# Two decoder layers with a mixture of experts on one core: half slots of the first gate weights get homes outside the ring

## The reference

```python
for l in range(DEPTH):                      # DEPTH = 2, SEQ = 256, D_MODEL = 1024
    h = rms_norm(x, norm_mix_g[l])
    x = x + token_mixers(h, ...)            # gMLP, sparse attention, short convolution, gated merge
    h = rms_norm(x, norm_ffn_g[l])
    x = x + hier_moe(h, ...)                # 4 groups of 8 experts, top-1 group, top-2 experts in it
return rms_norm(x, norm_final_g)

def expert_block(args):                     # one expert e, its tokens
    xb = xt[tok_b]
    hid = jax.nn.silu(xb @ w_gate[e]) * (xb @ w_up[e])   # 1024 x 512 each
    return hid @ w_down[e]                               # 512 x 1024
```

## Time and profile before

| | |
|---|---|
| median of 3 runs | 1394.22 us (1394.03 to 1395.34) |
| profiled execution | 1397.3 us, span 1395.6 us, granted clock 0.996 |
| busy share of the span | PE 98%, PEld 58%, DVE 41%, ACT 28% |
| moved by DMA | 490.27 MB, mean 351 GB/s |
| expert stage of layer 0 | PE starts it at 257.94 us |
| expert stage of layer 1 | PE starts it at 947.42 us |

### The profile page before, as it was taken

One profiled execution on the slowest core, in us unless ns is written; L12 is line 12 of the kernel. 1 busy time (PEld: TensorE's weight loads), 2 busy tenths in 40 slices (PEclk: granted clock), 3 DMA queues, 4 the chain that ended last, 5 costly groups with the idle time before them and its releaser, 6 DMA issues. The chain is left out here.

```text
span 1395.6 us, 18851 instructions
## 1 busy us (share of the span) xinstructions
PE 1366.0 (98%) x7854; PEld 810.0 (58%) x7854; DVE 574.1 (41%) x926; ACT 386.1 (28%) x709; POOL 6.3 (0%) x36
## 2 busy tenths in 40 slices
PE   8999999999999999999999999999999999999996
PEld 7899888644444444444488988884444444444332
DVE  6796646622222221212278956465222222222123
ACT  6554444211111111111164553441111111111112
POOL 0000000000000000000000000000000000000000
PEclk9999999999999999999999999999999999999999
DMA  8645757999999999999965557589999999999995
GB/s 311 218 164 185 279 199 275 403 421 428 428 428 427 426 426 428 427 427 419 405 220 184 211 188 265 189 352 386 425 428 427 427 428 427 427 427 426 426 420 243
DMA packets 86221, 490.27 MB, mean 351 GB/s; under 512 B 10303, under 2 KB 13433, under 8 KB 55417
## 3 DMA queue, kind: packets, MB, share of 16 engines
q1 hardware_dynamic: 86032, 489.03, 86.6%
q10 hardware_dynamic: 104, 0.03, 0.0%
HBM read 487.99 MB, written 1.05 MB: 350 GB/s over the span
## 5 line engine op out<-in xcount | busy, mean ns | idle before, releaser
L1984 PE MATMUL psB<-slots,uT 128*64 128x512 f32 x2048 | 459.8, 596 | 10.0 <-DMA slots<-in_expert_w_gate_dram 5.1
L1984 PEld LDWEIGHTS psB<-slots,uT 128*64 128x64 f32 x2048 | 143.7, 137 | 279.2 <-issue 275.6
L1994 PE MATMUL psC<-slots,ybT_plain 128*64 128x512 f32 x1024 | 227.2, 595 | 2.5 <-DMA slots<-in_expert_w_down_dram 1.6
L1124 DVE TENSOR_TENSOR parts<-slots,parts 128x2048 fp32r<-128x2048 f32 (+1 forms) x80 | 177.6, 2248 | 69.9 <-ACT parts L889 69.2
L889 ACT ACTIVATE parts<-slots 128x2048 fp32r<-128x2048 f32 (+1 forms) x80 | 148.3, 1888 | 97.2 <-PE psB L1653 52.7
L1500 DVE TENSOR_TENSOR x<-x,psA 128x1024 f32<-128x1024 f32 x62 | 75.7, 1221 | 227.7 <-PE psA L2031 227.7
L1994 PEld LDWEIGHTS psC<-slots,ybT_plain 128*64 128x64 f32 x1024 | 70.9, 137 | 133.3 <-issue 129.7
L996 ACT ACTIVATE rel_parts<-psC 128x512 fp32r<-128x512 f32 x62 | 37.0, 598 | 384.3 <-PE psC L1994 203.3
L1653 PE MATMUL psB<-parts,hT_parts 128*128 128x512 f32 x448 | 139.1, 392 | 1.5 <-DVE parts L1124 1.0
L1494 DVE TENSOR_TENSOR rel_parts<-psC,rel_parts 128x512 fp32r<-128x512 f32 x62 | 42.6, 688 | 163.8 <-ACT rel_parts L996 163.7
L1653 PE MATMUL psA<-parts,hT_parts 128*128 128x512 f32 x320 | 99.3, 391 | 0.0
(11 more groups left out here) (349 smaller groups left out, 1349.4 us busy)
## 6 DMA issues: line engine op xcount, KB each, us to landing
slots<-in_expert_w_down_dram SPq DMA_DIRECT2D x48, 2048.0 KB, 25.6
slots<-in_expert_w_gate_dram SPq DMA_DIRECT2D x44, 2048.0 KB, 25.7
slots<-in_expert_w_up_dram SPq DMA_DIRECT2D x44, 2048.0 KB, 24.8
slots<-in_w_in_dram SPq DMA_DIRECT2D x56, 1024.0 KB, 4.9
slots<-in_expert_w_gate_dram SPq DMA_DIRECT2D x40, 1024.0 KB, 13.0
slots<-in_expert_w_up_dram SPq DMA_DIRECT2D x40, 1024.0 KB, 13.6
slots<-in_expert_w_down_dram SPq DMA_DIRECT2D x24, 1024.0 KB, 19.1
slots<-in_w_out_dram SPq DMA_DIRECT2D x8, 1024.0 KB, 4.9
```

The lines of the kernel that those rows point to most:

```text
L1124: v.tensor_tensor(low_part, mix_slot(i), high_part, ALU.subtract).then_inc(low_dve, 1)
L1984: ins = te.matmul(psB[j * BLK:(j + 1) * BLK, o, :], xT[:, 4 * half + c, j * BLK:(j + 1) * BLK], w[:, c, :], start=half == 0 and c == 0, st ...
L1994: ins = te.matmul(psC[j * BLK:(j + 1) * BLK, n, :], hidT[:, 2 * k + c, j * BLK:(j + 1) * BLK], w[:, c, n * 512:(n + 1) * 512], start=k == ...
```

## The change

Three halves of gate slots of pair 0 get homes outside the ring: half 0 of load 0 in a new tile `first_rows`, half 0 of load 2 in `rel`, half 1 of load 3 in `ybT`. The freed half slots (half 0 of slots 0 and 2, half 1 of slot 3) take half of the down weights of pair 1 (loads 20, 22, 23). Stage 0 of pair 0 uses the chunks in the order 2, 3, 0, 1. `load_raw(35)` moves ahead of the wait for `merged_done`. The throw-away squares go to `uT`.

```diff
+        FIRST = {0: (sb("first_rows", [P, SLOT // 2]), 0),
+                 2: (nc.alloc_sbuf_tensor_at("first_in_rel", [P, SLOT // 2], F32, offset=place["rel"][0]), 0),
+                 3: (nc.alloc_sbuf_tensor_at("first_in_ybT", [P, SLOT // 2], F32, offset=place["ybT"][0]), 1)}
...
+                def load_first(n):
+                    home, piece = FIRST[n]
+                    load_piece(n, experts_of(0), home[:, :], piece, first_landed[n])
+                def load_early(s):
+                    n, piece = SLOTS + s, FIRST[s][1]
+                    load_piece(n % PAIR_SLOTS, experts_of(n // PAIR_SLOTS), half_slot(s, piece), piece, early_landed[s])
+                def load_rest(n):
+                    piece = 1 - FIRST[n % SLOTS][1]
+                    load_piece(n % PAIR_SLOTS, experts_of(n // PAIR_SLOTS), half_slot(n % SLOTS, piece), piece, landed[n % SLOTS])
...
                 def load_ahead(s):
...
+                    if s == 0:
+                        load_first(s)
+                    if s in FIRST:
+                        load_rest(s)
+                        return
                     load_main(s)
...
                 def load_high(i):
                     wait_used(sp, l, i)
+                    if high_slot(i) in FIRST:
+                        load_rest(high_slot(i))
+                        return
                     load_main(high_slot(i))
 
                 load_raw(MIX_SLOTS - 6)
+                wait_used(sp, l, USE[proj_of(2, 1), 0])
+                load_first(2)
+                load_raw(MIX_SLOTS - 5)
                 sp.wait_ge(merged_done, l * 2 + 2)
                 load_main(GATES_AT)
                 load_main(GATES_AT + 1)
-                load_raw(MIX_SLOTS - 5)
                 sp.wait_ge(merged_ps, l * 2 + 2)
                 load_main(MERGED_AT)
                 for i in range(MIX_SLOTS - 4, MIX_SLOTS):
                     load_high(i)
                     load_raw(i)
                 load_main(LOW_SLOT)
+                load_early(0)
+                load_early(2)
                 sp.wait_ge(route_ps, (l + 1) * NT)
                 load_main(HT_SLOT)
+                sp.wait_ge(low_x, (l + 1) * 2 * NT)
+                load_first(3)
+                load_early(3)
...
                             if n == SLOTS:
-                                load_pieces(p, experts, slots, [lambda: sp.wait_ge(early_freed, l + 1), lambda: wait_freed(n)], early_landed)
...
+                                sp.wait_ge(early_freed, l + 1)
+                                load_rest(SLOTS)
+                                load_rest(SLOTS + 2)
+                                continue
+                            wait_freed(n)
...
+                            for j in range(QB):
+                                if n + 2 * j == SLOTS + 3:
+                                    load_rest(n + 2 * j)
+                                    continue
+                                load_main(n + 2 * j)
...
-                        unread = (rel if half else uT)[:, :, :].rearrange("p h s -> p (h s)")[:, 512 * t:512 * t + 512]
+                        unread = uT[:, :, :].rearrange("p h s -> p (h s)")[:, 512 * t:512 * t + 512]
...
-                    for c in range(4):
-                        if first_pair and k == 0 and c == 2:
+                    opening = not tail and i == 0
+                    order = (2, 3, 0, 1) if opening and k == 0 else range(4)
+                    for c in order:
+                        if opening and k == 0 and c == 0:
                             ins.then_inc(early_freed, 1)
+                            pe.wait_ge(first_landed[0], (l + 1) * 16)
+                            pe.wait_ge(first_landed[2], (l + 1) * 16)
+                        if opening and k == 1 and c == 2:
+                            pe.wait_ge(first_landed[3], (l + 1) * 16)
                         for j in range(QB):
+                            home, piece = FIRST[at[j]] if opening and at[j] in FIRST else (None, None)
+                            if c // 2 == piece:
+                                w = home[:, c % 2 * 512:(c % 2 + 1) * 512]
+                            else:
+                                w = slot(at[j], SLOT)[:, c * 512:(c + 1) * 512]
...
                     if not tail and i * PAIR_SLOTS + part_of(4 + k, 0) == SLOTS:
-                        pe.wait_ge(early_landed, (l + 1) * 16 * QB)
+                        pe.wait_ge(early_landed[0], (l + 1) * 16)
+                        pe.wait_ge(early_landed[2], (l + 1) * 16)
+                    if not tail and i * PAIR_SLOTS + part_of(4 + k, 0) == SLOTS + 1:
+                        pe.wait_ge(early_landed[3], (l + 1) * 16)
```

More of the change, by code:

```diff
@@ L398, in build_trunk @@
         bidx = sb("bidx", [P, TAB_BLOCKS])
-        early_landed = sem("early_landed")
+        FIRST = {0: (sb("first_rows", [P, SLOT // 2]), 0),
+                 2: (nc.alloc_sbuf_tensor_at("first_in_rel", [P, SLOT // 2], F32, offset=place["rel"][0]), 0),
+                 3: (nc.alloc_sbuf_tensor_at("first_in_ybT", [P, SLOT // 2], F32, offset=place["ybT"][0]), 1)}
+        first_landed = {n: sem(f"first{n}_landed") for n in FIRST}
+        early_landed = {n: sem(f"early{n}_landed") for n in FIRST}
         early_freed = sem("early_freed")
@@ L625, in load_main, with experts_of, load_pieces @@
                     load_part(p, [l * NE + i * QB + j for j in range(QB)], n % SLOTS, doubled(n))
-                def load_pieces(first, experts, slots, waits, first_sem):
+                def experts_of(i):
+                    return [l * NE + i * QB + j for j in range(QB)]
+                def load_first(n):
[7 more added lines that the diff above has]
+                    load_piece(n % PAIR_SLOTS, experts_of(n // PAIR_SLOTS), half_slot(n % SLOTS, piece), piece, landed[n % SLOTS])
+                def load_pieces(first, experts, slots):
                     for piece in range(2):
-                        waits[piece]()
                         for j in range(QB):
-                            load_piece(first + 2 * j, experts, slots[j], piece, landed[slots[j]] if piece else first_sem)
+                            load_piece(first + 2 * j, experts, half_slot(slots[j], piece), piece, landed[slots[j]] if piece else tail_landed)
                 def load_ahead(s):
@@ L723, in sync_program @@
                             if k == STAGES - 1:
-                                load_pieces(part_of(k, 0), [l * NE + e for e in experts], [OVER_SLOTS[part_of(k, j)] for j in range(QB)],
-                                            [lambda: None, lambda: None], tail_landed)
+                                load_pieces(part_of(k, 0), [l * NE + e for e in experts], [OVER_SLOTS[part_of(k, j)] for j in range(QB)])
                                 continue
@@ L1977, in gate_up @@
                     at = [expert_arrived(i, part_of(k, j), tail) for j in range(QB)]
[L1978 to L1980 removed]
+                    opening = not tail and i == 0
+                    order = (2, 3, 0, 1) if opening and k == 0 else range(4)
+                    for c in order:
+                        if opening and k == 0 and c == 0:
                             ins.then_inc(early_freed, 1)
+                            pe.wait_ge(first_landed[0], (l + 1) * 16)
+                            pe.wait_ge(first_landed[2], (l + 1) * 16)
+                        if opening and k == 1 and c == 2:
+                            pe.wait_ge(first_landed[3], (l + 1) * 16)
                         for j in range(QB):
[L1983 to L1985 removed]
+                            home, piece = FIRST[at[j]] if opening and at[j] in FIRST else (None, None)
[3 more added lines that the diff above has]
+                                w = slot(at[j], SLOT)[:, c * 512:(c + 1) * 512]
+                            ins = te.matmul(psB[j * BLK:(j + 1) * BLK, o, :], xT[:, 4 * half + c, j * BLK:(j + 1) * BLK], w,
+                                            start=half == 0 and c == order[0], stop=half == 1 and c == 3)
                     ins.then_inc(pair_freed, 1)
```

24 lines of the change are left out of this document (11 added, 13 removed).

## The result

The changed kernel takes 1397.78 us in the median of 20 executions (1396.06 to 1400.33), the kernel before 1395.8 us beside it (20 executions, 1394.03 to 1398.79). The ratio is 1.0013, 95% interval [1.0007, 1.0019]. Two repetitions gave 1.0017 [1.0008, 1.0027] and 1.0011 [1.0001, 1.0021]. So the change costs 1.5 to 2.4 us (0.11 to 0.17% of 1396); a gain of 0.4 us was forecast. The size lies within what I had called no change (0.2%), but the sign holds in all three. The forecast time stood on the three executions of the kernel before that were there then, with a median of 1394.22 us; over 20 executions the kernel before has 1395.8 us, so of the 4.0 us between the forecast 1393.8 and the measured 1397.78 us, 1.6 us are the base, and 2.4 us lie between the forecast -0.4 and the measured +2.0 us.

The account below looks back on a forecast made before the run. The transfer stream's last byte was taken to end each expert stage. Layer 0: +0.4 stall, -0.3 slack, +0.1 us; layer 1: -0.5; together -0.4 from 1394.22 gives 1393.8 us, range 1389.5 to 1396.5.

Parts of the forecast that it names:

- what would show it: List of signs expected in the profile after: stretches filling, gaps in the stream, a PE wait, and limits for being wrong.
- the stretch 222 to 226 us: Nearly empty stretch of the stream in layer 0, at 10 GB/s, which should fill.
- a gap came ahead of load 32: Before load 32, at 290 to 292 us, the stream should show a gap that was not there.
- from load 32 on the rate is as before: The time from the issue of load 32 to the end of the layer should be as before.
- The gap at 264 to 266 us: Between the refills of stage 0 and stage 1, the stream should show a gap that was not there.
- PE's wait near 263 us: PE should wait for DMA about 0.4 us in layer 0; longer than 1.5 us would mean the forecast was wrong.
- Issues, squares and the other order of the chunks: Four more SP transfers per layer, squares written to `uT`, and gate matmuls in another order: all to cost nothing or be hidden.
- the new wait of PE: Stage 1, chunk 2: PE stalls for half 1 of load 3, 0.4 us in layer 0, none in layer 1.
- third rival: The wait in stage 1, chunk 2 grows as half slots flow slower: +2.1 us, 1396.3 us; chance 0.09.
- The slack at load 32: At load 32's issue the stream still has work queued, so 0.3 us in layer 0 and 0.5 in layer 1 are gained.
- The first rival: All 3.7 us per layer of bytes brought ahead arrive as gain: 1386.9 us; chance 0.10 for whole or most.
- the slowest-engine rival: The DMA engine ending the layer still has 1.2 us in stock at load 32, so gains more: 1391.4 us; chance 0.16.

Follow-up runs that it names:

- experiment 4: Kernel before with loads 32 to 67 issued one slot at a time: 1397.69 us; the same with loads 44 to 63 sent as two halves each: 1400.12 us.
- experiment 2: The change with half 1 of load 3 issued ahead of slot 18 instead of behind it: 1396.76 and 1397.07 us, ratios 0.9998 and 1.0001.

## Why the prediction was wrong

**The mechanisms were right, the sign was not.** Most of what was named in what would show it appeared: the stretch 222 to 226 us filled, a gap came ahead of load 32, PE waits for load 3's half, and from load 32 on the rate is as before (426 against 427 GB/s in layer 1). Two signs came otherwise. The gap at 264 to 266 us did not come there (324 against 317 GB/s) but at 267 to 272 us. And PE's wait near 263 us was 0, 0.9 and 1.6 us in three profiles; above 1.5 us I had called myself wrong. Issues, squares and the other order of the chunks cost nothing visible.

**The step that failed is the new wait of PE,** forecast as 0.4 us in layer 0 and 0 in layer 1. It measured 0, 0.9 and 1.6 us in layer 0 and 1.1, 1.0 and 1.3 us in layer 1 of the change's three profiles: 2.0 us together on average, 1.6 more than forecast; and each wait put load 32 off by 0.3 us more than itself. Two causes:

*Layer 1 was read against a disturbed start.* I set the half's landing, 952.0 us, against PE's need at 947.42 + 5.32. But that 947.42 was itself late. PE's timeline of the kernel before, with the same 30 small matmuls in layer 0 and in layer 1:

```profile
250.01 3.59 PE L1668 MATMUL psD<-ident,ones_r 128*128 128x128 f32 x30
...
938.21 5.22 PE L1668 MATMUL psD<-ident,ones_r 128*128 128x128 f32 x30
```

The same work took 1.6 us longer, with the granted clock of 938 to 944 us at 0.72, and stage 0 starts late: from the first scatter of layer 0's last pair (PE's matmul of `rel_parts` and `selT`) to stage 0 of layer 1 it is 252.61 us, against 251.28 in the profile after. The same distance in all 18 profiles of this case falls into two groups: 251.2 to 251.3 us in 14 of them, 252.6 to 252.7 us in four, of which one is the kernel before and three are versions of the change. So the 1.3 us come and go with the execution and not with the edit. In the profile after it is the other way round:

```profile
249.62 4.82 PE L1713 MATMUL psD<-ident,ones_r 128*128 128x128 f32 x30
...
937.60 3.59 PE L1713 MATMUL psD<-ident,ones_r 128*128 128x128 f32 x30
```

There layer 0 has the low clock (0.68 from 249 to 254 us), starts stage 0 late and needs no wait, and layer 1 is undisturbed and waits 1.06 us. The late half shows wherever PE comes on time: 952.0 against an undisturbed need some 1.3 us before 952.7 is a stall of 0.6 us, even with my own landing time.

*The half lands later than I put it.* From the start of stage 0 to its landing I had 263.7 - 257.94 = 5.8 us. In the five undisturbed layers of the change's profiles PE gets it 6.3 to 7.0 us after that start (in the third profile 265.32 against 258.32 us): 0.5 to 1.2 us later. (In the profile after it is there at 951.9 us in layer 1, where I had 952.0, but stage 0 began at 945.46 and not at 947.42 us.) Part of this is the stream ahead of it, 409 instead of 414 GB/s from 226 to 261 us, 0.4 us. I took half slots at 427 GB/s; at the 409 of experiment 4, three of them take 0.16 us longer. The rest is open. My third rival had half slots slower; its +2.1 us, for stalls of 1.6 and 0.5 us, were near what came, and I gave it 9 in 100. But its rate of 322 GB/s is not what half slots flow at (409), so its number was near by luck in part.

**The slack at load 32** was forecast to bring 0.3 and 0.5 us. It came, with more than that in layer 0. The length of an expert stage, from the start of stage 0 to the first scatter of the last pair, leaves out the scatter of the layer's start. The kernel before, then after, at these scatters:

```profile
694.81 0.50 PE L2030 MATMUL psA<-rel_parts,selT 128*128 128x512 f32 x1 [0.57 <-DVE rel_parts L1494]
...
1383.68 0.50 PE L2030 MATMUL psA<-rel_parts,selT 128*128 128x512 f32 x1 [0.56 <-DVE rel_parts L1494]
```

```profile
694.18 0.50 PE L2087 MATMUL psA<-rel_parts,selT 128*128 128x512 f32 x1 [0.56 <-DVE rel_parts L1539]
...
1382.83 0.50 PE L2087 MATMUL psA<-rel_parts,selT 128*128 128x512 f32 x1 [0.56 <-DVE rel_parts L1539]
```

| profile | layer 0, us | layer 1, us | both | PE's waits for the half |
|---|---|---|---|---|
| before | 436.9 | 436.3 | 873.1 | none |
| change | 435.7 | 437.4 | 873.0 | 1.1 |
| change again | 437.0 | 437.2 | 874.1 | 1.9 |
| change, third run | 437.7 | 437.4 | 875.2 | 2.9 |
| without the half, two runs | 436.2, 435.7 | 436.0, 435.9 | 872.2, 871.6 | none |
| half ahead, two runs | 436.6, 436.7 | 436.1, 436.0 | 872.6, 872.7 | none |
| third home alone | 437.8 | 438.0 | 875.8 | 3.3 |

The stages get longer with the waits, about us for us. Between the version with the half ahead and the one without it, the stages hold 0.4 to 1.1 us of the 2.2 us of experiment 2. From the issue of load 32 to the scatter the change is 1.0 to 1.3 us shorter than before in layer 0 and 0.2 to 0.4 us in layer 1, 1.4 us together: the stream had delivered that much more by then. The forecast had this as the slack, 0.8 us together. The comparison has one profile of the kernel before, so the 0.6 us between them may be its scatter. What no term of the sum had is that the rate of the stage's first 30 us is not a constant (experiment 2).

Adding up for the profiles, from the forecast -0.4 us: the waits and their 0.3 us put load 32 off by 2.4 us instead of 0.4, the slack brings 1.4 instead of 0.8, which makes +1.0 us; measured between the profiles' stages, +1.0 us in the mean. The times of all executions have +1.5 to +2.4 us by the ratios. The other 0.5 to 1.4 us are open. A likely place is the wait again: the first two profiled executions of the change, with waits of 1.1 and 1.9 us, took 1396.54 and 1396.66 us, well under the medians of their runs (1397.78 and 1398.23), and the third, with 2.9 us, took 1398.4 us, near its own (1398.14).

**The first rival** (the whole gain, 7.4 us) was rightly small: even with the home of load 3's half left out, 1.4 and 2.5 us arrive, and with load 32 freed as well 2.0 us twice. Nothing in the change's profiles speaks for the slowest-engine rival, and no run tested it by itself.

## What to carry to other kernels

Bytes brought ahead of a stage gain only as far as every later refill has slack; look for the next place where the stream runs dry before adding buffers. Here freeing that place (load 32) brought 2.8 and 3.0 us to the change and nothing to the kernel before. A part that moves from long landed to landing just before its use should be priced with the scatter of both times: here 0 to 1.6 us for one wait. Compare a stage's start between layers in the profile, relative to the same piece of work, before subtracting absolute times. The version to keep is the homes of loads 0 and 2 without that of load 3: 0.999 and 0.9982 as it is, 0.9986 [0.9977, 0.9995] in two runs with loads 32 to 43 one slot at a time. The runs don't tell these two apart.

## What the runs showed of the hardware

The rate of a full stream differed with its transfers: 427 GB/s with two slots (2 MB) a transfer, 422 with one, 409 with half, the last with rows of 4 KB, at the same or a higher DMA share. The size of a transfer and the length of its rows changed together there, so no run says which of the two it is. A stretch of whole slots can also flow at 390 to 413 GB/s instead of 419 to 423 at nearly the same share, some 10 to 25 us after the last half slot was issued. It did in the change and with the half moved ahead, and not with the home of load 3 alone (419 and 416) or without it (415 to 423). Whether the stream ran dry in between doesn't decide it: in the change's third run it did (274 GB/s at a share of 0.79 from 267 to 272 us), and 280 to 290 us still has 403; why stays open.

PE's granted clock falls for a few us around the small matmuls ahead of an expert stage in some layers of some executions, in versions with and without the change: a mean of 0.72 over 938 to 944 us of the kernel before and 0.68 over 249 to 254 us of the kernel after, between its levels of 1.2 and 2.4 GHz, and the 30 matmuls take 5.22 and 4.82 instead of 3.59 us. A start of the stage that differs by 1.3 us between two profiles is by itself no sign of an effect of the edit.
